# Experts of token block 0 chosen in two halves during the queries, with earlier gathers and more splits on GpSimd

## The reference

```python
qry = (xb @ w_q).reshape(TB, 8, 256)                  # xb: 128 tokens of h
s1 = einsum('thd,nd->thn', qry[..., :128], keys_1)    # 128 scores for each half key
s2 = einsum('thd,nd->thn', qry[..., 128:], keys_2)
v1, i1 = top_k(s1, 16); v2, i2 = top_k(s2, 16)
cand = (v1[..., :, None] + v2[..., None, :]).reshape(TB, 8, 256)
sc, ci = top_k(cand, 16)
idx = take(i1, ci // 16) * 128 + take(i2, ci % 16)    # 128 experts for each token
gate = softmax(sc)
act = gelu(einsum('thed,td->the', u_table[idx], xb))
y = einsum('the,thed->td', gate * act, v_table[idx])
```

## Time and profile before

| | |
|---|---|
| median of 3 runs (lowest, highest) | 1503.68 us (1499.63, 1505.55) |
| profiled execution | 1502.88 us, span 1501.1 us |
| busy | PE 98%, DVE 78%, POOL 45%, ACT 43% |
| mean granted PE clock | 0.991 |
| HBM | 410 MB moved, mean 273 GB/s |

### The profile page before, as it was taken

How to read it: one execution, slowest core, us unless ns; L and a number is a source line. 1 busy time by engine, 2 the same in 40 slices (tenths; PEclk the granted TensorE clock), 3 DMA queues, 4 the chain that set the end, 5 groups by cost and what they waited for, 6 DMA issues and landing times.

```text
span 1501.1 us, 23329 instructions
## 1 busy us (share of the span) xinstructions
PE 1467.1 (98%) x8045; PEld 1304.6 (87%) x8045; DVE 1174.9 (78%) x2373; ACT 640.7 (43%) x1055; POOL 672.8 (45%) x390
## 2 busy tenths in 40 slices
PE   7999989899999999999999999999999999999998
PEld 6879658788999999999999999988888888888887
DVE  4747473278999999989899899568878878877876
ACT  4463453222333333457777766433233233224221
POOL 2423140133586678865455454134433433443441
PEclk9999979999999999999999999999999999999999
DMA  7400202220569989999999999699999999999993
GB/s 263 148 29 1 113 1 74 85 85 16 191 224 351 328 307 351 412 376 358 370 366 375 373 358 387 238 378 376 386 350 354 346 347 352 347 352 349 350 344 123
DMA packets 183961, 410.28 MB, mean 273 GB/s; under 512 B 12852, under 2 KB 108852, under 8 KB 182360
## 3 DMA queue, kind: packets, MB, share of 16 engines
q1 hardware_dynamic: 142296, 258.46, 48.6%
q0 software_dynamic: 41600, 151.03, 26.5%
HBM read 361.12 MB, written 48.30 MB: 273 GB/s over the span
## 4 chain that ended last, share of the span: by engine, by line
PE 79%; DVE 9%; DMA 7%; POOL 2%; issue 1%; ACT 1%; SPq 0%; DVEq 0%; ACTq 0%; POOLq 0%
PE banks L1987 21%; PE banks L1760 16%; PE banks L2055 12%; PE banks L2056 12%; PE banks L2057 12%; DMA u_rows<-in_u,idx 7%; DVE gate_rows L1621 3%; DVE u_rows L1566 2%; POOL u_lo L739 2%; PE banks L2026 1%; PE banks L1968 1%; DVE u_lo L1549 1%; DVE oh L1617 1%; PE banks L1787 1%; PE banks L1832 1%
## 5 line engine op out<-in xcount | busy, mean ns | idle before, releaser
L787 POOL DMA_INDIRECT v_rows<-in_v,idx x128 | 204.2, 1596 | 325.5 <-DVE x_res L1705 273.9
L2055 PE MATMUL banks<-v_hi,w_hi 128*128 128x512 f32 x768 | 298.9, 389 | 0.0
L2056 PE MATMUL banks<-v_lo,w_hi 128*128 128x512 f32 x768 | 298.8, 389 | 0.0
L2057 PE MATMUL banks<-v_hi,w_lo 128*128 128x512 f32 x768 | 298.8, 389 | 0.0
L1118 ACT ACTIVATE v_hi<-v_raw 128x1024 fp32r<-128x1024 f32 x128 | 126.4, 1050 | 327.0 <-PE banks L2057 294.5
L755 POOL DMA_INDIRECT u_rows<-in_u,idx x160 | 189.2, 1182 | 137.6 <-DVE z L1566 105.2
L1643 DVE TENSOR_TENSOR v_lo<-v_raw,v_hi 128x1024 fp32r<-128x1024 f32 x128 | 153.4, 1219 | 96.3 <-ACT v_hi L1118 96.3
L739 POOL TENSOR_TENSOR u_lo<-u_raw,u_hi 128x1024 fp32r<-128x1024 f32 x66 | 164.6, 2497 | 86.4 <-ACT u_hi L1004 46.0
L1987 PE MATMUL banks<-h_lo,u_hi 128*128 128x352 f32 x1024 | 196.2, 326 | 0.0
L1987 PE MATMUL banks<-h_hi,u_hi 128*128 128x352 f32 x1024 | 189.2, 327 | 0.0
L1987 PE MATMUL banks<-h_hi,u_lo 128*128 128x352 f32 x1024 | 184.2, 322 | 2.8 <-DVE u_lo L1549 2.8
(11 more groups left out here) (277 smaller groups left out, 2086.9 us busy)
## 6 DMA issues: line engine op xcount, KB each, us to landing
u_raw<-in_uT SPq DMA_DIRECT2D x128, 512.0 KB
v_raw<-in_v SPq DMA_DIRECT2D x128, 512.0 KB
gate_scratch<-stage SPq DMA_DIRECT2D x12, 2048.0 KB
gates<-gate_scratch SPq DMA_DIRECT2D x29, 768.0 KB
act_scratch<-act_out SPq DMA_DIRECT2D x116, 176.0 KB
act_in<-act_scratch SPq DMA_DIRECT2D x29, 704.0 KB
wi_raw<-in_w_in SPq DMA_DIRECT2D x8, 1024.0 KB, 7.0
wq_raw<-in_w_q SPq DMA_DIRECT2D x8, 1024.0 KB, 5.7
```

The source lines that it names most:

```text
L787: nc.gpsimd.indirect_dma_start(v_rows[s % V_ROWS][:], None, v_flat, bass.IndirectOffsetOnAxis(ap=idx0[:, s:s + 1], axis=0)).then_inc(vg_in ...
L2055: mm(y, w, v_hi[q][:, j, ds], start=first and j == 0, stop=False)
L2056: mm(y, w, v_lo[q][j][:, ds], start=False, stop=False)
L2057: end = mm(y, w_lo[q][:, j, t * P:(t + 1) * P], v_hi[q][:, j, ds], start=False, stop=last and j == GROUP - 1)
```

## The change

The scores of a head now go into three banks: block 0 alone (`s0`, read by DVE), block 1 and blocks 2 and 3 (`s13`, copied to SBUF by ACT). DVE does in the queries the top-k of block 0 for all heads, of block 1 for seven heads and of block 2 for four; the rest, 13, move into the slots of the pre blocks. Block 0 is chosen in halves: heads 0 to 3 behind head 3's top-k, heads 4 to 7 in the first slots. POOL waits for the first half before the query split of head 7 and gathers from there; eight dots run in the queries. POOL splits blocks 0 to 31 and gathers between. DVE's slots begin at 0, with 2.65 us of pieces each up to slot 29, then 1.8. Several buffers move, `wq_lo` now lies over `wq_raw`, and so SP reloads it only when its query is done. The main blocks have three dots in slots 4, 8, 12, 16, 20, 24 and 32 to 42 by twos, where it was 4, 14, 24 and 32 to 44; the post blocks have none.

```diff
-POOL_FIRST, SHARE_FROM = 16, 20
+POOL_FIRST, SHARE_FROM = 32, 32
+EARLY = 8
+BANK_0 = 2
...
-DOTS = [""] * POST + ["aa"] * 4 + [""] * 4
+DOTS = [""] * E_BLOCKS
 for _n in range(POST):
     if _n + 2 in SHARED:
         DOTS[_n] = "aa"
-for _n in [*range(PRE - 25, PRE, 2), *range(PRE + 1, PRE + 32, 2), PRE + 4, PRE + 14, PRE + 24]:
+for _n in [x for x in range(30) if x % 3 < 2]:
+    DOTS[_n] = "a"
+for _n in [*range(PRE - 19, PRE, 2), *range(PRE + 1, PRE + 32, 2), *range(PRE + 4, PRE + 28, 4)]:
     DOTS[_n] += "b"
-for _n in [*range(PRE - 14, PRE, 4), *range(PRE + 32, POST)]:
+for _n in range(PRE + 32, PRE + 44):
     DOTS[_n] += "a"
...
+FREE_PIECE = 2650
 PIECE_SIZE = 1800
+TOPK_SIZE = 2900
+HALF_SIZES = (300, 1500, 500, 1600, 500, 1000, 400, 3350, 3350)
...
-        jobs += [(("s12", h, i), "D") for i in range(2)]
+        jobs += [(("s0", h), "D")] + [(("s13", h, i), "A") for i in range(2)]
...
+        scores_1 = at("scores_1", 186, [P, PH, 2 * NK])
+        scores_23 = at("scores_23", 150, [P, 2, PH, 2 * NK])
...
         def bank(job):
-            return ps[:, INDEX[job] % 8, :]
+            return ps[:, (INDEX[job] + BANK_0) % 8, :]
...
                 if h >= 3:
 
-                    sp.wait_ge(wqlo_ready, h - 2)
+                    arrived(sp, ("qry", h - 3, 1))
...
-            sp.wait_ge(wqlo_ready, PH)
-            load_u(0, 0)
             arrived(sp, ("qry", PH - 2, 1))
-            for j in range(1, 4):
-                load_u(j, j)
+            load_u(0, 0)
+            load_u(1, 1)
+            arrived(sp, ("qry", PH - 1, 1))
+            load_u(2, 2)
+            load_u(3, 3)
...
+            for h in range(PH - 1):
+                split_query(h)
+
+            pool.wait_ge(idx_ready, 1)
+            for s in range(U_ROWS // 2):
+                gather_u(s)
+            split_query(PH - 1)
+            for s in range(U_ROWS // 2, U_ROWS):
+                gather_u(s)
             for n in range(POOL_FIRST):
                 split_u(n)
-            pool.wait_ge(idx_ready, 1)
-            s = 0
+                if n < EARLY:
+                    gather_u(U_ROWS + n)
+                elif DOTS[n - EARLY]:
+                    gather_u(U_ROWS + dots_before(n - EARLY))
+            s = U_ROWS + dots_before(POOL_FIRST - EARLY)
...
+            take_query(0, 0)
+            take_query(0, 1)
+            round_q(2)
             for h in range(PH):
...
+                if h + 1 < PH:
+                    take_query(h + 1, 0)
+                j = ("s13", h, 0)
+                arrived(act, j)
+                free(copy(scores_1[:, h, :], bank(j)[:, 0:2 * NK]), j)
+                j = ("s13", h, 1)
+                arrived(act, j)
+                free(copy(scores_23[:, :, h, :], bank(j).rearrange("p (t e) -> p t e", t=2)), j)
+                if h + 1 < PH:
+                    take_query(h + 1, 1)
+                if h + 2 == PH:
+
+                    for b in (2, 3):
+                        emptied(act, LAST_ON[b])
+                    nc.scalar.activation(h2_first, h2_nat[:, 0, :], ACT.Copy).then_inc(h2_placed, 1)
+                if h + 3 < PH:
+                    round_q(h + 3)
+                if h + 2 == PH:
 
                     round_u(0, 0, True)
+                    round_u(1, 1, True)
...
-            for _ in choose(0):
+            for h in range(PH // 2):
+                top_k(0, h)
+                top_k(1, h)
+                if h:
+                    top_k(2, h - 1)
+            for _ in choose(0, 0, PH // 2):
                 pass
+            top_k(2, PH // 2 - 1)
+            for h in range(PH // 2, PH):
+                top_k(0, h)
+                if h > PH // 2:
+                    top_k(1, h - 1)
+                if h >= PH - 2:
+                    for _ in range(EARLY // 2):
+                        dot()
...
-            for n in range(POOL_FIRST - 2, PRE):
-                while done < (n - POOL_FIRST + 3) * PIECE_SIZE:
-                    done += next(sizes)
-                    next(work, None)
-                splits_and_dots(n)
+            work, done = routing(), 0
+            for n in range(PRE):
+                while done < min(n + 1, POOL_FIRST - 2) * FREE_PIECE + max(n - POOL_FIRST + 3, 0) * PIECE_SIZE:
+                    size = next(work, None)
+                    if size is None:
+                        break
+                    done += size
+                if n + 2 >= POOL_FIRST:
+                    splits_and_dots(n)
+                elif DOTS[n]:
+                    dot()
```

More of the change, by code:

```diff
@@ L176 @@
 ENGINE_OF = dict(JOBS)
+LAST_ON = [JOBS[max(n for n in range(len(JOBS)) if (n + BANK_0) % 8 == b)][0] for b in range(8)]
 NTH = {name: sum(e == eng for _, e in JOBS[: n + 1]) for n, (name, eng) in enumerate(JOBS)}
@@ L1491, in choose @@
                 settle()
-                for h in range(PH):
+                for h in range(h0, h1):
                     step(nc.vector.max(sc_v[:, t, h, 0:8], cand[:, h, :]))
@@ L1590, in splits_and_dots, with routing @@
                     dot()
-            work, done = itertools.chain(*(choose(t) for t in range(1, TB))), 0
-            sizes = itertools.cycle(CHOOSE_SIZES)
-            for n in range(POOL_FIRST - 2, PRE):
-                while done < (n - POOL_FIRST + 3) * PIECE_SIZE:
-                    done += next(sizes)
-                    next(work, None)
-                splits_and_dots(n)
+            def routing():
+                pieces = choose(0, PH // 2, PH)
+                for size in HALF_SIZES:
+                    next(pieces)
+                    yield size
+                assert next(pieces, 0) == 0
+                top_k(1, PH - 1)
+                yield TOPK_SIZE
+                for t in range(1, TB):
+                    if t > 1:
+                        for h in range(PH // 2 if t == 2 else 0, PH):
+                            top_k(t, h)
+                            yield TOPK_SIZE
+                    pieces = choose(t)
+                    for size in CHOOSE_SIZES:
+                        next(pieces)
+                        yield size
+                    assert next(pieces, 0) == 0
+            work, done = routing(), 0
[9 more added lines that the diff above has]
+                    dot()
                 if n == NORM_AT:
@@ L1961, in _ @@
                 emptied(pe, ("qry", h, 1))
[L1962 to L1964 removed]
+                for j, blocks in ((("s0", h), (0,)), (("s13", h, 0), (1,)), (("s13", h, 1), (2, 3))):
+                    o = start(j)
+                    for tt, t in enumerate(blocks):
                         for s in range(2):
                             c0 = (2 * tt + s) * NK
[L1967 removed]
                             last = mm(o[:, c0:c0 + NK], qryT[:, (2 * h + s) % 3, t * P:(t + 1) * P],
```

152 lines of the change are left out of this document (75 added, 77 removed).

## The result

The changed kernel takes 1542.85 us (median of 4 runs, 1540.57 to 1550.66). The kernel before took 1504.62 in the same comparison (4 runs, 1499.63 to 1506.37). The ratio is 1.0269, with a 95% interval of 1.0223 to 1.0314. The prediction was 1514.4 us with a range to 1532: the side was right, the size (+11.5 us) was under a third of what came. The profiled execution took 1544.65 us, its span 1542.9, 41.8 more than before.

A forecast was written before the change was run, and what follows sets the result against it. PE, busy 98%, bounds the kernel, with DVE second bound from 304 to 960. Terms 4.3 + 2.1 + 7.9 - 4.5 + 0 + 1.7 = +11.5 on 1502.9 give 1514.4 us; range 1495 to 1532.

The forecast's parts named there:

- stall of the second query of head 6: Queries: PE waits for its bank because POOL's query split holds DVE's half choice; 4.3 us, bounds 0 to 8.
- start of the first product: Before block 0: PE waits until ACT empties bank 0 of the last scores; 2.1 us, bounds 1 to 3.
- PE behind DVE (and POOL) in the first product: PE waits for DVE's late `u_lo` at slots 31 to 53; 7.9 us in all, bounds 0 to 11; POOL not added.
- wait at 960 and its slow clock: Late first product: no dots after block 117, so the 2.8 us wait and 1.7 us of slow clock go; -4.5 us.
- waits for `gate_rows`: Main blocks: three more dots against one cheaper slot; taken as 0, bounds -6 and +5.
- slow clock behind the new waits: One slow-clock stretch of PE behind a wait over 2.7 us; 1.7 us.
- pitch: First product's 352-column matmuls: no slower pitch counted in the forecast; 0.
- rival c: First product: pitch 1.34 instead of 1.27 from the first wait, 79 more blocks, +16 us, 1530 us; chance 0.12.
- I take 4: DVE's choices beside POOL's splits: the lock costs 4 us a choice, between readings of 1.8 and 5; 10 us for two and a half.
- at its edge too: POOL's 32 splits and 24 gathers need 111 to 130 us from 394; block 31 is needed at 516; not added.

The follow-up runs named there:

- second profile: The changed kernel run once more, unchanged, one run: 1542.09 us.
- The run with the two edits: Changed kernel with head 7's query split before POOL's wait for the indices and top-k (0,4) inside the half choice: 1534.84 us, ratio 1.0206.
- run with short splits: Changed kernel with POOL's splits of blocks 4 to 31 doing one of eight parts, the rest left out: 1512.28 us, ratio 1.0085.
- the order alone: Changed kernel with all top-k of blocks 1, 2 and 3 ahead of choices 1 to 3, pieces and queries as they are: 1527.47 us, ratio 1.011.
- two tries at a pause: Changed kernel with six already satisfied waits before each of POOL's 32 block splits, 1545.75 us; or a small memset between back-to-back splits, 1544.85 us.
- run with the choices late: Changed kernel with two query edits, early top-k of block 3, even 1950 ns pieces, and all top-k ahead of choices 1 to 3: 1507.58 us, ratio 1.0017.
- last try to beat both: Kernel with all top-k ahead of choices (1507.6), with `round_u(1, 1)` behind the last copies and four dots moved to slots 74 to 86: 1510.54 us, ratio 1.0003.

## Why the prediction was wrong, step by step

Of the 41.8 us, block 0 starts with 9.6 (398.8 against 389.2), blocks 0 to 32 bring 31.0, the rest of the first product 1.5, and the second product -0.3.

| step | predicted | measured |
|---|---|---|
| stall of the second query of head 6 | 4.3 | 4.5 |
| start of the first product | 2.1 | 1.5 |
| PE behind DVE (and POOL) in the first product | 7.9 | 25.1 |
| wait at 960 and its slow clock | -4.5 | -3.4 (1.05 us of the wait stay) |
| waits for `gate_rows` | 0 | -3.3 (+0.3 in the second profile) |
| slow clock behind the new waits | 1.7 | 5.9 |
| pitch | 0 (rival c: +16) | 10.8 (3.1 in the second profile) |
| before the queries' stall | 0 | 1.0 |

The terms measured in the first profile sum to 42.1 us, 0.3 over the 41.8.

- **The queries.** The mechanism was right in each link. POOL's split of 4.61 us started at 351.85, and DVE's `cand` at 352.06 took 5.03; the indices were ready at 368.9 (predicted 368.0). The run with the two edits removed it. (The row of a 2.42 us operation beside which the prediction cites the lock is a `TENSOR_SCALAR` with one input; `cand`, with two, is the nearer example.)
- **The lag: the step that failed.** "I take 4, because POOL now splits every block up to 31 and gathers between." The price is 32 us for two and a half choices (138.9 less 106.8; the run with short splits took 106.9), 13 each. So this term, put at 10 us, was mis-sized by 22. The 4 was read where POOL was ahead of PE and paused for ACT. Here it was late, pairs of its splits stood without a pause, and each hold delayed a dot that its next gather needed: it fell back further. The run with short splits took the cost away and left the rest; the order alone took 17 us of it. Besides, DVE's slot 0 began at 411.3, not at 408.0.
- The place was near: block 32, not 33. I had expected the first 6.7 us there and it was 17.8; the other 7.3 were POOL's own lateness in blocks 18 to 31, which the prediction saw ("at its edge too") and did not add.
- **The clock.** The prediction counted one stretch at half clock and there were three. By the rows above, behind the waits of 4.51, 2.43 and 17.79 us the matmuls lose 2.5, 1.6 and 1.8 us until they are back at full speed (3.55 and 2.60 for 1.82; 2.15 and 2.08 for 1.34; 2.52 and 1.80 for 1.27). The length of a wait does not set the price behind it, nor does it tell whether there is one: the prediction took a stretch behind each wait over 2.7 us, but the wait of 2.43 us at 501 was followed by one, and the wait of 2.46 us at 472.5 was not (the next groups stand 1.44 and 1.33 us apart).
- **The pitch.** 69 blocks (counted in groups of eight matmuls) at 0.2 us more (24 matmuls at 167 ns instead of 158), where the profile of before had 15. Rival (c) gave this a chance of 0.12 as something that the first wait sets off for good. It isn't for good (blocks 33 to 65 ran at 158), and it falls both ways: in both profiles of the changed kernel the product came out of the long wait at block 32 at 158, in the two tries at a pause at 167.
- **Gates.** The expected zero came out as a gain of 3.3 in the first profile, but the second profile of the same kernel has 3.6 us of these waits. The pitch goes with it. Of the twelve profiles of the changed kernel and its variants three have no wait for `gate_rows` (the first one, the queries' run, the order alone), and these are the three in which blocks 72 to 119 are slow from end to end; the others have 1.7 to 6.7 us. That a slower PE gives DVE the time it lacks is the likely reason, and no run forces it. So the two terms belong together: -3.3 and 10.8 in the one profile, +0.3 and 3.1 in the other.

The Trainium skill, page "SBUF — State Buffer", section "SBUF: two separate sides", was cited for a lock that is held for a whole instruction. The traces agree and go further: in the 8.26 and 12.49 us VectorE was held for two and five instructions. The same section, under "Who interferes with whom", lets through an operation with at most one input from SBUF outside the two-port modes. The top-k at 286 ns beside full splits agree (a `MATCH_VALUE_LOAD` of its own stands before each `FIND_INDEX8`), and the run with the choices late rests on that. One input alone was not enough: the casts `tri` (1506 ns for 224) and `idx` (3620 for 190) and the copy `tops` (1785 for 167) were held. The section names copies and casts among the operations that can enter such a mode; no run here shows in which mode they ran.

## What to carry to other kernels

Price an operation of DVE that GpSimd can hold by the chain of GpSimd operations that can stand in a row beside it, not by one of them, and read that price from a stretch in which GpSimd is as late as it will be. Where work can be ordered freely, find in the trace which operations keep their time beside GpSimd (here the top-k operations, the `TENSOR_REDUCE`, and the dots with one operand in PSUM), put these beside its dense stretches, and put what is held (here the operations with two inputs from SBUF, the casts and the copy) where it pauses: this was worth 15 us in each of two kernels without an instruction less. Here a lag that no wait showed was paid at the first place where the critical engine met the late one (block 16 or block 32).

## What was not expected of the hardware

- VectorE held for 12.49 us by five GpSimd operations in a row, with a 0.1 us memset between two no relief.
- Waits on the queue of GpSimd that are already satisfied cost its engine nothing that the trace shows: with six of them before each split, pairs of splits still took 4.76 us.
- The 352-column matmuls have two pitches at full clock, 158 and 167 ns, and change between them almost only where PE's stream is broken (a wait, the gate matmuls, the transposes at block 66); once, at 518.91 in the first profile, where no wait is listed. The same program falls differently from run to run. In the third comparison the kernel before itself spread from 1499.4 to 1520.3 us at a granted clock of 0.988 to 0.992; the pitch may be the reason, but those runs have no profile. Against that spread, the last try to beat both and the kernel before can't be told apart. The kernel with the choices late was measured in a calmer comparison, and there its interval (1.0005 to 1.003) lies just above 1. No version was shown to be faster than the kernel before.
